# A decoder layer on one core: a quarter of the experts' first products computed in an earlier stage, three stages joined

## What is computed

```
q = (xi @ wq).reshape(PEER_TOKEN_BLOCK, PEER_HEADS, 2, PEER_DKEY // 2)
s = jnp.einsum('nhcd,ckd->nhck', q, subkeys, preferred_element_type=jnp.float32)
sv, si = lax.top_k(s, K)
...
top_s, pos = lax.top_k(cand, K)
eid = jnp.take_along_axis(cid, pos, axis=-1)
g = jax.nn.softmax(top_s, axis=-1)
hpre = jnp.einsum('nd,nhkd->nhk', xi, u_tab[eid], preferred_element_type=jnp.float32)
a = (jax.nn.gelu(hpre, approximate=False) * g).astype(xi.dtype)
return jnp.einsum('nhk,nhkd->nd', a, v_tab[eid])
```

## Time and profile before

| | |
|---|---|
| time of the profiled execution | 2648.93 us |
| its span (first to last instruction) | 2647.1 us |
| median of the three timed runs | 2651.59 us |
| PE busy | 2289.9 us (87% of the span) |
| DVE busy | 1610.1 us (61%) |
| ACT busy | 928.9 us (35%) |
| bytes moved | 555.47 MB, mean 210 GB/s |
| mean granted TensorE clock | 0.917 |

### The profile page before, as it was taken

One profiled execution on the slowest core, in us unless ns is written; L12 is line 12 of the kernel. 1 busy time (PEld: TensorE's weight loads), 2 busy tenths in 40 slices (PEclk: granted clock), 3 DMA queues, 4 the chain that ended last, 5 costly groups with the idle time before them and its releaser, 6 DMA issues.

```text
span 2647.1 us, 38437 instructions
## 1 busy us (share of the span) xinstructions
PE 2289.9 (87%) x13177; PEld 1955.8 (74%) x13177; DVE 1610.1 (61%) x3159; ACT 928.9 (35%) x1417; POOL 359.4 (14%) x370
## 2 busy tenths in 40 slices
PE   7997879998997989504376999999999999999994
PEld 7996656666664469503376999999999999999993
DVE  3433322343434347799994667777677776777767
ACT  3225533444445122102263333333333333333331
POOL 0000000000000000100000223222232222322230
PEclk9998879899988989856687999999999999999997
DMA  3220026667665111299965888888787887878873
GB/s 121 91 73 33 1 91 200 201 207 225 198 201 190 64 48 49 80 323 339 364 263 201 278 274 283 275 281 278 272 284 275 282 278 273 285 273 282 278 273 105
DMA packets 214837, 555.47 MB, mean 210 GB/s; under 512 B 16993, under 2 KB 87202, under 8 KB 212066
## 3 DMA queue, kind: packets, MB, share of 16 engines
q1 hardware_dynamic: 165730, 315.16, 36.3%
q0 software_dynamic: 49024, 239.23, 25.4%
HBM read 521.95 MB, written 98.83 MB: 235 GB/s over the span
## 4 chain that ended last, share of the span: by engine, by line
PE 68%; DVE 10%; DMA 5%; SPq 2%; ACT 2%; issue 1%; POOLq 0%; DVEq 0%; ACTq 0%; POOL 0%
PE psum L1913 20%; PE psum L1925 19%; PE psum L1523 4%; PE psum L1903 4%; DMA gates_dram<-gate_table 3%; PE psum L978 3%; PE psum L1386 3%; PE psum L1050 2%; PE psum L1032 2%; DVE gate_table L1726 2%; PE psum L968 2%; PE psum L1000 2%; DMA sample<-in_cache_v_sb_dram 2%; DVE gate_table L1723 1%; PE psum L1766 1%
## 5 line engine op out<-in xcount | busy, mean ns | idle before, releaser
L1913 PE MATMUL psum<-h_parts,expert_parts 128*128 128x384 f32 x3072 | 592.9, 341 | 4.2 <-DVE expert_parts L2013 4.2
L1925 PE MATMUL psum<-expert_parts 128*128 128x512 f32 x2304 | 557.2, 395 | 0.0
L1913 PEld LDWEIGHTS psum<-h_parts,expert_parts 128*128 128x128 f32 x3072 | 537.7, 189 | 14.6 <-DVE expert_parts L2013 4.8
L1925 PEld LDWEIGHTS psum<-expert_parts 128*128 128x128 f32 x2304 | 423.3, 188 | 83.5
L2013 DVE TENSOR_TENSOR expert_parts<-psum,expert_parts 128x512 fp32r<-128x512 f32 x256 | 177.1, 692 | 293.2 <-ACT expert_parts L1955 293.2
L1961 ACT ACTIVATE expert_parts<-peer 128x1024 fp32r<-128x1024 f32 x128 | 135.8, 1061 | 365.9 <-PE psum L1925 365.9
L1955 ACT ACTIVATE expert_parts<-psum 128x512 fp32r<-128x512 f32 x256 | 153.1, 598 | 200.5 <-PE psum L1903 200.5
L2053 DVE SCALAR_TENSOR_TENSOR kept<-experts,kept 128x1024 f32<-128x1024 f32 x160 | 204.7, 1280 | 3.9 <-DVE kept L2043 2.8
L1305 DVE TENSOR_TENSOR sample_parts<-sample,sample_parts 128x512 fp32r<-128x512 f32 x128 | 85.2, 690 | 158.0 <-ACT sample_parts L1158 158.0
L394 PE MATMUL psum<-projection_parts 128*128 128x256 f32 (+1 forms) x1440 | 173.7, 282 | 3.8 <-DVE projection_parts L500 3.8
L1883 POOL DMA_INDIRECT experts<-in_peer_u_dram,kept x96 | 113.0, 1178 | 468.5 <-DVE experts L2037 345.4
(11 more groups left out here) (271 smaller groups left out, 2993.7 us busy)
## 6 DMA issues: line engine op xcount, KB each, us to landing
peer<-in_peer_u_dram SPq DMA_DIRECT2D x128, 512.0 KB, 5.6
peer<-in_peer_v_dram SPq DMA_DIRECT2D x128, 512.0 KB, 3.7
sample<-in_cache_k_sb_dram SPq DMA_DIRECT2D x128, 256.0 KB, 3.1
sample<-in_cache_v_sb_dram SPq DMA_DIRECT2D x128, 256.0 KB, 3.0
out_dram<-in_state_k_win_dram POOLq DMA_DIRECT2D x8, 4088.0 KB, 104.9
out_dram<-in_state_v_win_dram POOLq DMA_DIRECT2D x8, 4088.0 KB, 118.2
gates_dram<-gate_table SPq DMA_DIRECT2D x12, 2048.0 KB, 8.4
experts<-gates_dram SPq DMA_DIRECT2D x32, 768.0 KB, 6.0
```

The source lines that it names most:

```text
L1913: last = pe.matmul(bank(6)[:, 0:ND], lhsT=u_t[s][:, a, k, :], rhs=h1_r[:, b, k, 0:ND], start=(k == 0 and n == 0), stop=(k == KD - 1 and n ...
L1925: last = pe.matmul(bank(2 * t + half), lhsT=weight[s][:, a, t * P:(t + 1) * P], rhs=v_r[s][:, b, half * 512:(half + 1) * 512], start=(firs ...
```

## The change

1. **Early blocks.** Every fourth block (x = 4e+3, e from 0 to 31) has its u loaded, transposed and multiplied with the rows in the queries' and gate tables' part of the program: 8 transposes and 8 whole-f32 products of 128x384 (`turn_early`, `hidden_early`) in place of 24 f32r products. ACT copies and makes the gelu, and SP stores it to `gelu_dram`. In the experts' loop these blocks have no `hidden` and no `turn_u`; SP loads their gelu (192 KB), and the rest is as before. An f32 copy of the rows (`h1_f`) costs six more ACT copies in the stage of the first norm. The order on PE, ACT and SP is written by `gate_schedule`: blocks 0 to 11 ahead of turn(0), 12 to 16 ahead of turn(1), 17 to 19 inside chunks 1 to 3, 20 to 24 ahead of turn(2), 25 to 31 inside chunks 4 to 10. The exponentials of top_k go behind blocks 1, 5, 10, 15 and 22 on ACT.
2. **Barriers.** There is none behind the queries, the gate tables and the experts; waits on single semaphores stand in their place.
3. **Table chunks** use six PSUM banks in thirds, not eight in quarters; the loops over chunks are written out.
4. **u loads** of the next full block stand ahead of the v load of this block in SP's program.
5. **Gathered rows**: in set q the adds of set q and the dots of set q+1 are made; the first set makes two sets of dots, and nothing stands behind the last block.
6. **State copies** go out in four lots of 7, 4, 3 and 2, at the start of the two prompt attention stages, of the first-norm stage and of the queries.
7. **The query products** are 384 and 256 columns in place of twice 320.
8. **The end** norms the gathered tile and the sample rows first; each dense tile waits for its own products (`y_tile`).

The core of the diff:

```diff
+        MOVES = (7, 4, 3, 2)
+
+        def move_state(pool, turn):
+            for n in range(sum(MOVES[:turn]), sum(MOVES[:turn + 1])):
+                b = n // 2
+                to, frm = ((k_win_sample, state_k_win), (v_win_sample, state_v_win))[n % 2]
+                pool.dma_start(to[b].rearrange("w h d -> (w h d)")[0:(WIN - DT) * DH],
+                               frm[b].rearrange("w h d -> (w h d)")[DT * DH:WIN * DH]).then_inc(sem("window_moved"), 16)
...
+            pool.wait_ge(sem("counts_in"), 2 * 16)
+            move_state(pool, 0)
...
+                    if t < NTD:
+                        act.activation(h1_f[:, 4 * half:4 * half + 4, t * P:(t + 1) * P],
+                                       bank(4 + u % 4).rearrange("p (k n) -> p k n", k=4), ACT.Copy)
+                    act.activation(h1_tile(0, slice(4 * half, 4 * half + 4), t),
                                    bank(4 + u % 4).rearrange("p (k n) -> p k n", k=4), ACT.Copy).then_inc(sem("h1_high"), 1)
...
+        EXP_AFTER = {1: 0, 5: 1, 10: 2, 15: 3, 22: 4}
+        BLOCK_OF = {1: 17, 2: 18, 3: 19, 4: 25, 5: 26, 6: 27, 7: 28, 8: 29, 9: 30, 10: 31}
+        FIRST_OF = ((0, 12), (12, 17), (20, 25))
...
+        def gate_schedule(turn, block, chunk):
+
+            for t in range(NTD + 1):
+                if t < NTD:
+                    for e in range(*FIRST_OF[t]):
+                        block(e)
+                    turn(t)
+                if t >= 1:
+                    for c in range(TILE_CHUNKS * (t - 1), TILE_CHUNKS * t):
+                        chunk(c, BLOCK_OF.get(c))
...
+                if e is not None:
+                    block(e)
+                sp.wait_ge(sem("table_copied"), 4 * c + 7)
+                sp.dma_start(gates_dram[c], table[c % 2].rearrange("p i n -> p (i n)")).then_inc(sem(f"table_out_{c % 2}"), 16)
...
+            def turn_early(e, half):
+                if e == SETS:
+                    return
+                if half == 0:
+                    pe.wait_ge(sem(f"early_in_{e % 2}"), 16 * (e // 2) + 16)
+                pe.wait_ge(sem("early_copied"), 2 * e + half)
+                for k in range(4):
+                    last = pe.transpose(bank(7)[:, k * P:(k + 1) * P], early_u[e % 2][:, 4 * half + k, :], ident)
+                last.then_inc(sem("early_turned"), 1)
+
+            def hidden_early(e, half):
+                pe.wait_ge(sem("early_copied"), 2 * e + half + 1)
+                if half == 0 and e >= 1:
+                    pe.wait_ge(sem("early_gelu"), e)
+                elif half == 0:
+                    pe.wait_ge(sem("sample_scores"), 1)
+                for k in range(4 * half, 4 * half + 4):
+                    last = pe.matmul(bank(6)[:, 0:ND], lhsT=early_t[e % 2][:, k, :], rhs=h1_f[:, k, :],
+                                     start=(k == 0), stop=(k == KD - 1))
+                if half == 1:
+                    last.then_inc(sem("early_hidden"), 1)
+
+            def block_half(e, half):
+                turn_early(e + 1, half)
+                hidden_early(e, half)
...
+            def chunk(c, e):
+                if c % TILE_CHUNKS == 0:
+                    pe.wait_ge(sem("ijg_turned"), min(c // TILE_CHUNKS + 2, NTD))
                 for half in range(2):
                     pe.wait_ge(sem("hot_ready"), 4 * c + 2 * half + 2)
-                    for n in range(HALF_C):
-                        if n % 8 == 0:
-                            pe.wait_ge(sem("table_copied"), 4 * c + 2 * half + n // 8 + 1)
...
+                    for q in range(2 * half, 2 * half + 2):
+                        r = 4 * c + q
+                        pe.wait_ge(sem("table_copied"), r + 1)
+                        for n in range(QUARTER):
+                            at = q % 2 * QUARTER + n
+                            last = pe.matmul(bank(2 * (r % 3) + n // 4)[:, n % 4 * NK:(n % 4 + 1) * NK],
+                                             lhsT=hot_j[half][:, at, :], rhs=hot_i[half][:, at, :], start=True, stop=True)
+                        last.then_inc(sem("table_ready"), 1)
+                    if e is not None:
+                        block_half(e, half)
...
+            def gelu_early(e):
+                act.wait_ge(sem("early_hidden"), e + 1)
+                if e >= 2:
+                    act.wait_ge(sem(f"early_out_{e % 2}"), 16 * (e // 2))
+                act.activation(early_gelu[e % 2], bank(6)[:, 0:ND], ACT.Gelu).then_inc(sem("early_gelu"), 1)
+
+            def exponents(e):
+                if e in EXP_AFTER:
+                    act.wait_ge(sem("best_less"), EXP_AFTER[e] + 1)
                     act.activation(gate_e, gate_e, ACT.Exp).then_inc(sem("gate_exp"), 1)
...
+            def block(e):
+                if e >= 1:
+                    gelu_early(e - 1)
+                copy_early(e + 1, 0)
+                copy_early(e + 1, 1)
+                exponents(e)
...
+        def is_full(k):
+            return k % SET != SET - 1
...
+                    if is_full(k) and not is_last(turn, k) and not (isinstance(turn, int) and turn == 0 and k == 0):
+                        j = full_of(k) + 1
+                        after = x + 1 if is_full(k + 1) else x + 2
+                        sp.wait_ge(sem("u_turned"), 2 * (FULL * turn + j) + 2)
+                        sp.dma_start(u_sb[j % 2], peer_u[bass.ds(after * P, P), :]).then_inc(sem(f"u_in_{j % 2}"), 16)
                     if not (isinstance(turn, int) and turn == 0 and k < 2):
-                        sp.wait_ge(sem("u_turned"), 2 * x + 2)
-                        sp.dma_start(u_sb[k % 2], peer_u[bass.ds(x * P, P), :]).then_inc(sem(f"u_in_{k % 2}"), 16)
                         sp.wait_ge(sem("v_low"), x + 1)
                         sp.dma_start(v_sb[k % 2], peer_v[bass.ds(x * P, P), :]).then_inc(sem(f"v_in_{k % 2}"), 16)
...
+            pe.wait_ge(sem("early_copied"), 2 * SETS)
             turn_u(0, 0, 0, 0)
             turn_u(0, 0, 0, 1)
+            pe.wait_ge(sem("early_gelu"), SETS)
...
+                    if is_full(k):
+                        j = full_of(k)
+                        f = FULL * turn + j
+                        for half in range(2):
+                            hidden(f, j % 2, half)
+                            if not is_last(turn, k):
+                                turn_u(f + 1, 1 - j % 2, FULL // 2 * turn + (j + 1) // 2, half)
                     if not (isinstance(turn, int) and turn == 0 and k == 0):
                         add_up(x - 1, 1 - s, first=isinstance(turn, int) and turn == 0 and k == 1)
 
             over_turns(pe, blocks)
+            pe.wait_ge(sem("added"), PLACES * SETS)
+            pe.wait_ge(sem("gelu_done"), SETS * (SET - 1) + 2)
+            pe.wait_ge(sem("u_low"), 2 * SETS * (SET - 1) + 2)
+            for half in range(2):
+                last = pe.matmul(bank(6 + half)[0:NS, :], lhsT=pick, rhs=y_s[:, half * 512:(half + 1) * 512], start=True, stop=True)
+            last.then_inc(sem("f_turned"), 1)
             add_up(NK - 1, 1, final=True)
...
+            for e in range(2):
+                act.wait_ge(sem(f"early_out_{e}"), 16 * (SETS // 2))
...
+                    if full:
+                        u_low(f + 1, 1 - e, 0)
+                    if r in (1, 2) and not first:
+                        add(q, r + 1)
+                    gate(x, turn, k)
+                    if full:
+                        u_low(f + 1, 1 - e, 1)
+                    weight_low(x, s, k)
                     v_low(x, s)
-                    if before and r == 0:
-                        rows_gate(q - 1)
-                        add(q - 1, 0)
-                    if before and r == 3:
-                        add(q - 1, 4)
-                    for p in ((0,), (1,), (2, 3), (4,))[r]:
-                        dot(q, p)
+                    if first:
+                        for p in ((0, 1, 2), (3, 4), (), ())[r]:
+                            dot(0, p)
+                    if r == (2 if first else 0):
+                        rows_gate(q)
+                        add(q, 0)
+                        add(q, 1)
+                    if first and r == 3:
+                        add(q, 2)
+                        add(q, 3)
+                    if r == (2 if final else 3):
+                        add(q, 4)
+                    if not final:
+                        for p in ((), (), (0, 1), (2, 3, 4))[r] if first else ((0,), (1, 2), (3,), (4,))[r]:
+                            dot(q + 1, p)
 
...
+        LAST_ORDER = (NTD, NT - 1) + tuple(range(NTD))
...
-            for t in range(NT):
+            dve.wait_ge(sem("added"), PLACES * SETS)
+            for i, t in enumerate(LAST_ORDER):
...
+                if t < NTD:
+                    dve.wait_ge(sem("y_tile"), t + 1)
```

280 lines of the change are left out of this document (161 added, 119 removed).

## The result

| | before | after |
|---|---|---|
| median of four timed runs | 2650.11 us | 2492.64 us (2491.88 to 2493.82) |
| profiled execution, span | 2647.1 us | 2491.4 us |
| mean granted TensorE clock | 0.917 | 0.952 |

A forecast was written before the change was run, and what follows sets the result against it. PE was taken to bound the experts' loop, DVE the gate stage where PE stood idle. Terms of -160 + 6 - 5 + 4 - 12 = -167 took 2648.9 to 2482 us, range 2455 to 2535.

The forecast's parts named there:

- Term 1: Experts' loop: 32 early blocks each save the 5.01 us of hidden and transposes, -160 us.
- Term 2: Fourth block of each set: only 1.0 us to spare before the second add_up; 0.2 lost a set, +6 us.
- Term 4: First set of the loop: DVE makes ten dots and five adds instead of five dots, +4 us, bounds 0 and 12.
- Term 3: Gate tables and experts' start: early blocks fit PE's idle time, tables end as before, seam 29 us; -5 us.
- Term 5: End: DVE norms gathered tile and sample rows during the last products; 33.5 us instead of 45.7, -12 us.
- At nothing: state copies: Copies in attention, first-norm and query stages: covered by stage length, no cost; otherwise one load waits up to 13 us, once.
- within 10 us of 1411: Sign that the forecast is right: the gate stage's table products end within 10 us of 1411 us.
- No barrier behind the queries: at nothing: Between queries and gate tables: removing the barrier wins nothing, since DVE works 109.14 of the 110 us behind it.
- A (short blocks): Loop: DVE sets the short blocks, an add and a dot late every set; 42 instead of 6, 2518 us; chance 0.12.
- B (314 GB/s needed): Loop: DMA engines become the bound if they sustain less than 314 GB/s; at 290, +86, 2568 us; chance 0.12.
- C (clock): Gate tables: PE stays at the lower clock, early blocks cut by waits; 237 us more, 2719 us; chance 0.04.
- D: Loop keeps its pace because the freed 5 us are not used; 2640 us; chance 0.02.

The follow-up runs named there:

- run 4: The changed kernel without early blocks: all 128 blocks have their first products in the experts' loop, all other edits stay; 2642.3 us.
- run 6: The changed kernel with ACT's last early gelu and its store ahead of the last table chunk's copies; median 2489.0 us, ratio to before 0.9390.
- run 2: The changed kernel with all 16 state copies in lots of 6, 4, 3, 1, 1, 1, behind the loads in first-norm stage and queries; 2485.4 us, timed again median 2477.2.
- Runs 1: The changed kernel with the 16 state copies left out; 2484.2 us.
- run 9: The changed kernel with the barrier of all engines behind the queries put back; 2517.4 us.

## Why the prediction was right, and where its steps failed

- **Term 1, the loop (-160): right.** A set is 36.76 us without and 31.65 with early blocks, so 32 early blocks save 32 x 5.11 = 163.5 us. Run 4 gives 159.1 for the loop, because the first set loses more with early blocks than without them (term 4).
- **Term 2 (+6): nothing.** The sets take 31.65 us, and PE is busy for 440.00 of 440 us: no short cover was too short. The 1.0 us to spare was enough: behind the first set PE never waited for DVE.
- **Term 4 (+4): the mechanism right, the size half of it.** The first set takes 40.38 us in place of 31.65, 8.7 more, inside the bound of 12: PE waits 6.15 us for a u_low behind DVE's extra dots and adds, and the add_up behind the wait is 2 us slower. Without early blocks, with the same dots and adds, the first set loses only 4.3 (41.08 against 36.76).
- **Term 3 (-5): right in its number, -7, in part by luck.** The stage takes 313.8 us from the queries' end (315 forecast) and the seam 27.6 (29). PE's layout held: an early block takes 6.5 us (6.4). But that the stage ends where it did is a balance that I had not forecast: by run 4 the early blocks cost it 5.5 us, and the other edits win 7.5. In the seam, too, the early blocks give back 4.9 of 10.0 us, since the last gelu's store sets it (run 6).
- **Term 5 (-12): right,** 33.5 us by its own steps: 3.4 to the first residual (3.6), 30.1 for norms and store (29.9).
- **"At nothing: state copies": wrong, 18.5 us.** The step said "their cover is the length of those stages; without it a load waits behind one copy, up to 13 us, once". But a load waited behind more than one copy: the 512 KB issued 0.1 us behind the first of three landed 31.3 us later, at 909.0, with the second copy (909.2) and ahead of the third (922.1); with the copies behind the loads it took 5.2 us (run 2). It happened in two stages, and a barrier opened only when the copies had landed. Runs 1 and 2 remove it at each of the three places. By this the tables ended at 1427.9, outside the "within 10 us of 1411" that the prediction named as a sign.
- **"No barrier behind the queries: at nothing"** was right only beside the old work: run 9 prices it at 12.7 us. Term 3 had silently used it, as it let PE begin at 1095.
- **The sum.** -163.5 + 0 - 7.1 + 8.7 - 12.2 + 18.5 are -155.6, the difference of the spans within rounding. The forecast came within 11 us although 23 us were missed (the copies and term 4), because terms 1, 2 and 3 gave 12 more than forecast; that they met is luck. The lower end of the range is added up wrongly as well: 2482 less 6, 4, 12 and 8 are 2452, not 2455.
- **Rivals.** A (short blocks): behind the first set no wait is to be seen. B (314 GB/s needed): the loop moved 306 to 320 GB/s at shares of 0.90 and 0.93 without making PE wait for a load. C (clock): 0.97 and 0.99. D: 31.65 us a set.
- **The table loads.** Behind four of the five exponentials PE waits 1.18 us for the next gelu, in most other places 0.24, so there and back costs PE 0.94 us; behind the first it waits 4.82, since that exponential waits for top_k's numbers. The first 12 blocks took 90 us in place of 88. The Trainium skill, "ScalarE: Activation LUTs", section "What ACT_TABLE_LOAD costs", gives a drain of about 1.38 us beside each load; by it, an estimate, ten switches would have added 14 us. The trace does not show the drain: at 1161.71 us ACT loads a table for 1.28 us and begins the exponential at 1163.01.

## What to carry to other kernels

A stage in which one engine is full and another idle is room for the idle engine's work from elsewhere, even at a worse price (6.5 us there for 5.1 in the loop), if it is laid out against the full engine's turns. What has been resting in such a stage, as bulk copies or barriers, must then be priced again: it was free, or nearly so, only beside the old work. Bulk copies go behind a stage's loads, and land before its barrier.

## What was not expected of the hardware

- Loads issued in the same microsecond as copies of 4,088 KB on another queue came in with or behind the copies: 512 KB in 31.3 us (5.2 with the copies behind it), 1 MB in 48.2 (10.0); an early u beside sixteen copies in 47.5 (3.6). The load issued 0.3 us ahead of the first copy took 4.5. Why is not shown; in the queries the copies' queue moved 8.37 MB in 160 packets, the loads' queue 7.34 MB in 6,528.
- The barrier ahead of the second attention opened when POOL's last copy had landed: PE went on at 307.5 to 311.9 us in the eight profiles with seven copies there, 0.4 us behind the landing of the seventh in each, and at 304.0 to 306.3 in those with six or none, 0.5 us behind the last work of PE, ACT and DVE. Which engine's part of the barrier waits was not tried.
- With half the early products PE was busy for 72.16 of 110 us in the first part of the gate stage, and its clock was granted at 0.84, against 0.97 at 97.67: less work, at a lower pace.
